# Half-integer spectrum, folded transforms, and twelve projection chunks around the convolution in a two-block kernel

## The reference, cut to what matters

```python
def bidirectional_long_conv(v, h_fwd, h_bwd):
    length = v.shape[1]                      # 256
    n_fft = 2 * length                       # 512
    k = jnp.concatenate([h_fwd, zeros(1), h_bwd[:0:-1]], axis=0)
    v_f = jnp.fft.rfft(v, n=n_fft, axis=1)
    k_f = jnp.fft.rfft(k, n=n_fft, axis=0)
    return jnp.fft.irfft(v_f * k_f[None], n=n_fft, axis=1)[:, :length]

def hyena_mix(u, conv_w, conv_b, ..., bias):
    x0, x1, v = jnp.split(short_conv(u, conv_w, conv_b), 3, axis=-1)   # 512 features each
    v = v * x1
    h_fwd, h_bwd = hyena_filter(length, ...)
    y = bidirectional_long_conv(v, h_fwd, h_bwd) + v * bias
    return y * x0
```

## Time and profile before

| what | value |
|---|---|
| median of 3 runs | 1920.15 us (1918.99 to 1921.41) |
| profiled execution, span from first to last instruction | 1919.0 us, mean granted PE clock 0.991 |
| PE busy | 1873.1 us, 98% of the span |
| DVE, ACT, POOL busy | 1002.7, 796.4, 123.6 us |
| share of PE in the chain that ended last | 88% |

### The profile page before, as it was taken

How to read it: one execution, slowest core, us unless ns; L and a number is a source line. 1 busy time by engine, 2 the same in 40 slices (tenths; PEclk the granted TensorE clock), 3 DMA queues, 4 the chain that set the end, 5 groups by cost and what they waited for, 6 DMA issues and landing times.

```text
span 1919.0 us, 27635 instructions
## 1 busy us (share of the span) xinstructions
PE 1873.1 (98%) x11404; PEld 1584.8 (83%) x11404; DVE 1002.7 (52%) x1210; ACT 796.4 (41%) x1000; POOL 123.6 (6%) x116
## 2 busy tenths in 40 slices
PE   7999999999999999999999999999999989999998
PEld 6779895888987888767888778888887977988898
DVE  5756565587655336753434422223226585556664
ACT  6434435454445433354323422223225435355553
POOL 3000111300013001000000100000001010000000
PEclk9999999999999999999999999999999999999999
DMA  9986476776533322133234243332365421556751
GB/s 282 301 262 236 138 267 244 234 202 208 184 132 113 102 88 88 56 121 106 88 102 118 67 110 93 91 106 88 118 232 176 132 66 56 186 154 176 196 197 66
DMA packets 296877, 287.02 MB, mean 150 GB/s; under 512 B 8860, under 2 KB 273715, under 8 KB 291660
## 3 DMA queue, kind: packets, MB, share of 16 engines
q1 hardware_dynamic: 294440, 279.88, 46.0%
q0 software_dynamic: 2112, 5.68, 1.0%
q10 hardware_dynamic: 227, 0.06, 0.0%
HBM read 283.07 MB, written 2.38 MB: 149 GB/s over the span
## 4 chain that ended last, share of the span: by engine, by line
PE 88%; DVE 4%; POOL 3%; ACT 2%; DMA 1%; issue 1%; ACTq 0%; SPq 0%; POOLq 0%; DVEq 0%
PE PS L1793 19%; PE PS L1794 19%; PE PS L1795 19%; PE PS L1838 12%; PE PS L1839 6%; PE PS L2446 2%; PE PS L1974 1%; POOL SQ L634 1%; POOL X L650 1%; PE PS L2434 1%; PE PS L2407 1%; PE PS L2472 1%; DMA RAW<-in_w_in_dram 1%; PE PS L2394 1%; PE PS L2253 1%
## 5 line engine op out<-in xcount | busy, mean ns | idle before, releaser
L1150 DVE TENSOR_TENSOR WLO<-RAW,WHI 128x2048 fp32r<-128x2048 f32 x209 | 483.8, 2316 | 377.8 <-ACT WHI L702 377.5
L702 ACT ACTIVATE WHI<-RAW 128x2048 fp32r<-128x2048 f32 x209 | 398.8, 1909 | 261.4 <-PE PS L1795 237.7
L1793 PE MATMUL PS<-AHL,WHI 128*128 128x512 f32 (+1 forms) x1424 | 487.5, 342 | 2.3 <-DVE AHL L1257 2.0
L1794 PE MATMUL PS<-AHL,WHI 128*128 128x512 f32 (+1 forms) x1424 | 481.8, 338 | 0.0
L1795 PE MATMUL PS<-AHL,WLO 128*128 128x512 f32 (+1 forms) x1424 | 481.7, 338 | 0.0
L1838 PE MATMUL PS<-AHL,WHI 128*128 128x512 f32 x1056 | 376.2, 400 | 4.1 <-DVE AHL L1257 2.1
L1793 PEld LDWEIGHTS PS<-AHL,WHI 128*128 128x128 f32 x1424 | 270.7, 190 | 37.3 <-issue 6.3
L1839 PE MATMUL PS<-AHL,WLO 128*128 128x256 f32 x1056 | 296.5, 281 | 0.0
L1794 PEld LDWEIGHTS PS<-AHL,WHI 128*128 128x128 f32 x1424 | 270.8, 190 | 29.9 <-issue 1.4
L1795 PEld LDWEIGHTS PS<-AHL,WLO 128*128 128x128 f32 x1424 | 270.8, 190 | 28.7
L1838 PEld LDWEIGHTS PS<-AHL,WHI 128*128 128x128 f32 x1056 | 200.1, 189 | 61.8 <-issue 14.1
(11 more groups left out here) (290 smaller groups left out, 1925.7 us busy)
## 6 DMA issues: line engine op xcount, KB each, us to landing
RAW<-in_w_in_dram SPq DMA_DIRECT2D x98, 512.0 KB, 4.5
RAW<-in_ffn_w_gu_dram SPq DMA_DIRECT2D x88, 512.0 KB, 6.3
RAW<-in_w_gate_up_dram SPq DMA_DIRECT2D x88, 512.0 KB, 4.9
MRAW<-in_w_mod_dram SPq DMA_DIRECT2D x32, 1024.0 KB, 7.2
RAW<-in_ffn_w_down_dram SPq DMA_DIRECT2D x44, 512.0 KB, 4.2
RAW<-in_w_down_dram SPq DMA_DIRECT2D x44, 512.0 KB, 4.0
RAW<-in_w_out_dram SPq DMA_DIRECT2D x24, 512.0 KB, 4.5
RAW<-in_w_o_attn_dram SPq DMA_DIRECT2D x16, 512.0 KB, 4.2
```

The costliest lines, as they stand in the source:

```text
L702: act.activation(WHI[:, c % RING, :], RAW[:, c % RING, :], ACT.Copy).then_inc(S("hi_done"), 1)
L1150: dve.tensor_tensor(WLO[:, c % RING, :], RAW[:, c % RING, :], WHI[:, c % RING, :].bitcast(F32), ALU.subtract)\
L1793: pe.matmul(out, whi, xhi, start=first, stop=False, skip_group_check=shared)
L1794: pe.matmul(out, whi, xlo, start=False, stop=False, skip_group_check=shared)
```

## The change

The spectrum is taken at half-integer frequencies (k + 1/2). It has then no real-only first and middle value, so KRX and the two fix-up operations (`nyquist`) go. A sequence of 256 tokens is folded: POOL forms sums and differences UD of each token with its mirror image (128 each); the transform of 256 tokens by 512 values splits into two of 128 by 256. The same split, backwards, is in the inverse. The filters' sum and difference are taken of `filt_w4` itself on POOL (`tap_weights`), so that a spectrum tile needs one direction only, and the bias is added to the filter's tap 0. The twelve chunks of a layer are one stage "win" in a new order: v's and x1's four hy chunks, keys and values, x0's two hy chunks, queries. The transforms stand between and within the later chunks.

```diff
-STAGES += [(f"qkv{_l}", 6), (f"hy{_l}", 6), ...
+STAGES += [(f"win{_l}", 12), ...
-HY_ORDER = (2, 3, 4, 5, 0, 1)
-S_BANK = ((2, 2, 2, 7), (4, 6, 7, 6))
+WIN = (("hy", 4), ("hy", 6), ("hy", 8), ("hy", 10), ("kv", 8), ("kv", 10),
+       ("hy", 0), ("hy", 2), ("q", 0), ("q", 2), ("q", 4), ("q", 6))
+WIN_BANK = (0, 2, 4, 6, 0, 2, 0, 2, 0, 2, 0, 2)
+GROUPS = (2, 1)
+S_BANK = ((2, 7, 4, 3), (4, 5, 7, 6))
 # POOL, per layer, ahead of the rotations
+pool.wait_ge(S("hy_v"), HT * (layer + 1))
+for g in range(GROUPS[layer]):
+    front = HY[:, 8:12, TX * g:TX * g + P]
+    back = HY[:, 8:12, TX * g + P:TX * g + TX][:, :, ::-1]
+    for r, op in enumerate((ALU.add, ALU.subtract)):
+        pool.tensor_tensor(UD[:, g, r, :, :], front, back, op).then_inc(S("y_ud"), 1)
 # ACT: ple_gate, then the win stage
-            spectrum_out(0, 0)          # in ple_gate, j == 0
-                spectrum_out(0, 1)
-            spectrum_out(0, 2)          # behind norm_std(7, 2)
+            spectrum_out(0, 0)          # behind norm_std(7, 2)
+            spectrum_out(0, 1)
+                for q, (kind, m0) in enumerate(WIN):
+                    split_w(None, c + AHEAD)
+                    if q == 5:
+                        for g in range(GROUPS[layer]):
+                            turned_out(g)
+                        key_roots()
...
+                    act.wait_ge(S("pe_done"), c + 1)
+                    if kind == "hy":
+                        hyena_tiles(q, m0)
...
                     if layer == 0 and q == 0:
+                        spectrum_out(0, 2)
                         spectrum_out(0, 3)
                     if layer == 1 and q == 0:
                         late_rows(MAIN + HALVES + 8, MROW2)
+                    if layer == 1 and q in (1, 2):
                         ctx_modulated(2, 0, 0, range(4 * q - 4, 4 * q))
 # DVE: a unit's spectra are six operations of 512, convolved three; win stage
+                for q, (kind, m0) in enumerate(WIN):
+                    split_w(None, FIRST[f"win{layer}"] + q + AHEAD)
...
+                        if q in (1, 2):                      # layer 1
+                            ctx_low(2, range(4 * q - 4, 4 * q))
+                        elif q == 3:
+                            late_columns(1, 3, 2)
...
+                    if kind == "hy":
+                        tapped(q, m0)
...
 maxima(0)
-convolved(last_y - 1)
-convolved(last_y)
+rotated(4)
 # PE
 for j in range(4):                       # ple_gate
     ...
-    if j == 0:
-        spectrum_tile(0, range(4))
     if j == 1:
         norm_sum_added(3, 6)
-        spectrum_tile(1, range(4))
 norm_sums(7, 2, SQ1, range(2, 4))
-pe.wait_ge(S("f_ev"), 5)
-spare(5, 5)
+spectrum_tile(0)
 norm_sums(7, 2, SQ1, range(4, 6))
-spectrum_tile(2, range(2))
+spectrum_tile(1)
 norm_sums(7, 2, SQ1, range(6, KT))
...
+def forward(y):                          # 4 matmuls of 256 columns
+    for ct in range(CTILES):
+        last = pe.matmul(PS[...], FOLD[:, ct * P:ct * P + P], VTT[g][:, ct // 2, TX * h:TX * h + TX], start=True, stop=True)
+def inverse(y):                          # 8 matmuls of 128 columns
+    for m in range(2):
+        for r in range(2):
+            for a in range(2):
+                last = pe.matmul(PS[:, 6, ...], YS[:, h, 2 * r + a, m * P:m * P + P], UNFOLD[:, 2 * r + a, :], ...)
+def within(q):                           # between a chunk's two output tiles
+    if layer == 0:
+        if q == 5: turned(1); key_sums()
+        elif q == 6: key_rows()
+        elif 7 <= q <= 10: inverse(q - 7)
+    else:
+        if q == 5: key_sums(); forward(0)
+        elif q == 6: key_rows(); forward(1)
+        elif q == 8: inverse(1)
+    if 9 <= q <= 11: query_sums(q - 9)
+def behind(q):
+    if q == 4: turned(0)
+    if layer == 0 and 5 <= q <= 8: forward(q - 5)
+    if layer == 1 and q == 2: mod_turn(3, 1, MROW2)
+    if layer == 1 and q == 6: inverse(0)
+for q, (kind, m0) in enumerate(WIN):
+    if layer == 0 and q == 1:
+        pe.wait_ge(S("s_ev"), 4)
...
+    if layer == 1 and q == 4:
+        pe.wait_ge(S("ctx_lo"), 3 * KT)
+        pe.wait_ge(S("mod_ev"), 12)
-pe.wait_ge(S("h_sum"), 5 * (layer + 1))
 scores2(0)
-inverse(last_y - 1)
-inverse(last_y)
+query_sums(3)
...
-                    if layer == 0 and i is None and j < 3:    # gu0
-                        later_spectrum(j + 1, range(4))
+                    if layer == 0 and i is None and j < 2:
+                        later_spectrum(j + 2)
```

More of the change, by code:

```diff
@@ L575, in _ @@
                 win = d["w_in_2"][layer]
-                for j in range(6):
+                for j, (kind, m) in enumerate(WIN):
                     if layer == 1 and j < 2:
@@ L579, in _ @@
                             late_load(n)
[L580 removed]
+                    load(None, FIRST[f"win{layer}"] + j, cols(win, (12 + m if kind == "hy" else m) * P), by_k(KT))
                     if j == 2:
                         tables(layer)
[L583 to L584 removed]
                 woh = d["w_o_hyena_2"][layer].rearrange("(k p) n -> p k n", p=P)
@@ L669, in _ @@
             add_squares(2, 4)
+            tap_weights(0)
             x_update(2)
@@ new lines, in _ @@
+                    if q == 4:
+                        act.wait_ge(S("qkv_ev"), 6 * layer + 1)
+                        act.activation(HSQ[:, :, :], QKV[:, 8:10, :], ACT.Square).then_inc(S("h_sq"), 1)
+                    if kind == "q":
+                        query_pair(m0 // 2)
+                    if layer == 0 and q == 0:
+                        spectrum_out(0, 2)
+                        spectrum_out(0, 3)
+                    if layer == 1 and q == 0:
+                        late_rows(MAIN + HALVES + 8, MROW2)
@@ L1857, in network @@
                 if l == 0:
-                    pe.wait_ge(S(("filter", "late")[layer]), 96)
+                    pe.wait_ge(S(("filter", "late")[layer]), 112)
                     if layer == 1:
@@ L2381, in _, with turned @@
-                groups = nt // TX
-                def forward(y):
-                    h = y % 2
-                    y += 4 * layer
-                    pe.wait_ge(S("y_vt"), y // 2 + 1)
-                    if y >= 4 * layer + 2:
-                        pe.wait_ge(S("y_mul"), 7 * (y - 1))
-                    else:
-                        pe.wait_ge(S("hy_taps"), 24 * layer + 20 + 4 * h)
+                def turned(g):
+                    ud0 = 2 * sum(GROUPS[:layer])
+                    pe.wait_ge(S("y_ud"), ud0 + 2 * g + 2)
+                    if g:
+                        pe.wait_ge(S("y_vt"), sum(GROUPS[:layer]) + g)
+                    for r in range(2):
+                        for m in range(HT):
+                            last = pe.transpose(PS[:, 4 + r, m * P:m * P + P], UD[:, g, r, m, :], IDENT[:, :])
+                    last.then_inc(S("y_tr"), 1)
@@ new lines, in behind @@
+                def behind(q):
+                    if q == 4:
+                        turned(0)
+                    if layer == 0 and 5 <= q <= 8:
+                        forward(q - 5)
+                    if layer == 1 and q == 2:
+                        mod_turn(3, 1, MROW2)
+                    if layer == 1 and q == 6:
+                        inverse(0)
+                for q, (kind, m0) in enumerate(WIN):
+                    c, n = FIRST[f"win{layer}"] + q, win_n(layer, q)
+                    out = win_out(layer, q)
+                    outs = [out[:, 0, :], out[:, 1, :]]
+                    if layer == 0 and q == 1:
+                        pe.wait_ge(S("s_ev"), 4)
+                    if q in (4, 5):
+                        pe.wait_ge(S("hy_taps"), 24 * layer + 4 * (q - 3))
+                    elif q in (6, 7):
+                        pe.wait_ge(S("qkv_ev"), 6 * layer + q - 5)
+                    elif q in (8, 9):
+                        pe.wait_ge(S("hy_taps"), 24 * layer + 4 * (q - 3))
+                    elif q >= 10:
+                        pe.wait_ge(S("qkv_ev"), 6 * layer + q - 7)
+                    if layer == 1 and q == 4:
+                        pe.wait_ge(S("ctx_lo"), 3 * KT)
+                        pe.wait_ge(S("mod_ev"), 12)
+                    if q == 0 and layer == 0:
+                        by_halves(c, outs, AHI2, ALO2, ("act_lo", 5 * KT), ("ctx_lo", 0))
+                    elif q == 0:
+                        by_columns(None, c, outs, AHI2, ALO2, n, ready=wait_k("act_lo", KT * (5 + 2 * layer)))
+                    else:
+                        by_columns(None, c, outs, AHI2, ALO2, n, between=lambda last: within(q))
+                    behind(q)
```

535 lines of the change are left out of this document (257 added, 278 removed).

## The result

| | before | with the change |
|---|---|---|
| median of four runs each | 1919.74 us (1918.99 to 1921.41) | 1900.35 us (1899.71 to 1901.92) |
| profiled execution, span | 1919.0 us | 1898.4 us, mean granted clock 0.987 |
| ratio of the medians | | 0.9898 (95% interval 0.9886 to 0.9910) |

A forecast was written before the change was run, and what follows sets the result against it. PE, busy 98% of the span, was taken as the bound. Layer 0 +9.7, layer 1 +5.3, filter spectrum +6.9 and +0.8, clock -7.6 sum to +15.1: span 1903.9, median 1905, range 1892 to 1916.

The forecast's parts named there:

- gu0 at +6.9: Behind gu0's start, three filter spectrum tiles become two of half the length, 10.3 to 3.4, all on PE's path: +6.9.
- The rule of narrow matmuls: Skill's ratio against the forecast's 128-column price: an inverse takes 2.5 instead of 1.72, six cost 4.7 more, 1910.
- the rival of the weight loads: Rival 2: weight loads pace narrow matmuls; an inverse takes 2.2, six cost +3.0, 1908 in all; chance 0.1.
- (a): Layer 0, ahead of chunk 1: PE waits until ACT has copied spectrum tiles out of the banks; -2.8.
- (c): Layer 1, ahead of chunk 4: PE waits for the modulation's columns, which DVE computes behind earlier chunks' taps; -4.4.
- The wait for POOL's UD: Sign of being wrong: PE waits at `turned` for POOL's sums and differences; cost set to nothing, cover 1.2.
- (b): Layer 0's first softmax, with no transforms to fill it: lasts 14.8, PE has 8.6 of work and stands 6.2; -6.2.
- (d): Layer 1's first softmax, filled as in layer 0's: 14.2, less 7.8 of PE's own work; -6.4.
- Rival 4: Both layers' softmax fills are as long as the transforms they replace, 4 longer each, 8 together: 1913; chance 0.1.
- the clock, -7.6: Half clock after four new waits, in ple_gate, layer 0's chunk 1, layer 1's chunk 4 and softmax: 4 x 1.9.
- Filter spectrum in ple_gate: Two tiles lose 3.4 each beside POOL's and DVE's work: +0.8, 0.2 behind the gate, 0.6 at the norms' sums.
- rival 3: DVE paces layer 1's chunks and the kernel gets slower: 8.2 a chunk loses the gain, 9.1 gives 1929; chance 0.1.

The follow-up runs named there:

- the doubling runs: Changed kernel with every forward transform's four matmuls issued twice, 1909.57 us; separately, every inverse transform's eight 128-column matmuls issued twice, 1910.81 us.
- the fourth: Changed kernel with the last query pair rotated behind the second maxima instead of between first maxima and first normalisation: median 1900.21 us.

## Why the prediction was right, and where it was off

- **Prices.** Forward and inverse at 1.72, gu0 at +6.9, PE busy down to 1840: they measured 1.73 and 1.78, 6.95 and 1838.4, and the doubling runs show +6.91 and +3.39 where 6.9 and 3.4 were in the sum.
- **The rule of narrow matmuls.** By the ratio of the Trainium skill, page "TensorE: Matmul & The Clock Gate", section "Back-to-back issue gap", an inverse would have taken 2.5. The trace has 1.78 for one and 3.57 for two, so here, in float32 with two instructions a matmul, the rule does not decide. It and the rival of the weight loads (2.2) are out.
- **Waits (a) and (c).** 2.5 for 2.8, 4.1 for 4.4, each with the releaser named. The runs that reordered ACT or DVE alone took (c) away wholly and left 0.57 of (a). The wait for POOL's UD, which the prediction named as a sign of being wrong, did not come: `turned` waited for nothing.
- **The softmax fills (b) and (d).** 15.3 and 14.9 for 14.8 and 14.2 to the first values: the chain was right to 0.7. What filled it was not: in layer 0 PE stood 2.84 and not 6.2, and worked the more, at half clock. Rival 4, fills 4 longer each, did not happen.
- **The term that failed is the clock, -7.6.** It was mis-sized in four ways. (1) "Each time it did, PE lost 1.93", counted for (a): the wait of 2.51 lost nothing here, and in two of the eight edited kernels that keep it it lost 1.3 to 1.8. (2) In (d) I took 1.9 for the clock on top of a fill whose length comes from a chain through ACT and DVE: counted twice. With idle matmuls in its place the stage moved by 0.6 only. (3) Behind (c) it came to 1.3, by the run that took that wait away. (4) I wrote that the attention before started at full speed after 1.92 and ended my comparison at the first values. That was misread: its first values already took 2.42 instead of 1.9, the granted clock was 0.50 at 807, and 6.1 passed to the second values instead of 4.3, another 1.8 that went. Together 1.9 + 1.9 + 0.6 + 1.8 = 6.2, less 1.2 for the longer fills, and 0.6 for the shorter waits: 5.6, as much as the two layers brought above the forecast. These are rounded terms from single executions, so that they meet to the tenth is partly luck. What decides whether the clock falls at a given wait stays open.
- **Filter spectrum in ple_gate.** Forecast +0.8 - 1.9, measured -1.7. The clock came as forecast (1.93 by the run with idle matmuls). Of the 0.8 only 0.2 came, all of it at the norms' sums: behind the gate PE starts 24.28 after the stage's start, before it was 24.22. A third wait, 1.2 for WLO behind chunk 0, which I had missed, cost nothing, since POOL's sum behind it starts 20.50 after the stage's start, before it was 20.45.
- **DVE as the bound of layer 1 (rival 3).** It did not happen, and my reason (no iteration is longer than PE's by much) holds, with about 2.8 to spare by the run with more work on DVE.

## What to carry to other kernels

A transform or copy that stands where PE waits anyway costs nothing, and making it shorter there gives nothing; look at what ends the wait before counting the saved matmuls. When work is moved out of a latency-bound stretch (a first softmax), its cover goes with it: write down the chain through ACT and DVE first, and then what PE has left. After such a change, go through the new waits one by one: here three edits of a few lines, two in the order of single engines and one of idle matmuls, gave half as much again as the change itself, and the fourth added nothing that the median shows.

## What the hardware showed that I had not expected

The same wait with the same work around it kept the clock in one execution and lost it in another: 2.51 ahead of chunk 1, full clock in the changed kernel, 0.50 for about 3.5 us in the run with ple_gate's idle matmuls and in the one with inverses twice. The Trainium skill, page "TensorE: Matmul & The Clock Gate", part 1, says that the monitor behind the clock runs free of the kernel and that the point at which it switches varies from run to run. These rows agree in that one wait came out both ways; they do not show why. In a sum, a wait of 2.5 is then a chance of 1.3 to 1.8, not a price.

Second, with identical instructions, the stretch from layer 1's fourth values to the end took 327.3 to 327.6 in seven of the fourteen profiled executions (before among them), 328.2 to 328.3 in three, and 329.65 to 330.56 in four. In the windows around layer 1's last norm the granted clock was 0.50 for some 3.5 us in the seven and for about 7 in the three, which fits the 0.8 between them. Of the four, the run with more work on DVE (329.65) was at 0.50 for some 10 us there and ran like the changed kernel behind it. The other three (330.5 to 330.6) have some 2 us that the clock does not explain, spread evenly over the stage behind the norm: 88 matmuls take 15.55 from start to start where they take 15.25 in the changed kernel, and this from the stage's second eighth to its end. Windows of 30 us, PE busy throughout at clock 1.00, hold 175 matmuls in the changed kernel and 172 in the run with the late rotation:

```profile
1735.00:1765.00 30.00, 30.00 (x175) 1.00 0.67 186
```

```profile
1735.00:1765.00 30.00, 30.00 (x172) 1.00 0.65 177
```

Why is open. It means that a gain of 1 us is to be read from stages here, since single executions of one kernel differ by 3 and more (1908.61 to 1915.43 with inverses twice).
